# Splitting the first mixer's first weights ahead of the modulation, and putting the attention products ahead of the convolution's layer norm, in a two-block float32 kernel

## The reference

```python
mod = c_act @ w_ada[l] + b_ada[l]
sh1, sc1, ga1, sh2, sc2, ga2 = jnp.split(mod, N_MOD, axis=-1)
u = modulate(rmsnorm(h, g_norm1[l]), sh1, sc1)
...
proj = u @ w_in
p_conv, q, k, v, r, a1, gates = jnp.split(proj, offs, axis=-1)
y_conv = conv_module(p_conv, ...)      # depthwise, width 31, then layernorm, silu, @ w_pw
o = gla_chunked(q, k, v, logg)         # gated linear attention, 4 heads, value width 256
o = rmsnorm(o, g_gla_norm...)
y_gla = (o * jax.nn.silu(r)) @ w_gla_o
gt = jax.nn.sigmoid(gates)
merged = gt[:, :, 0, :] * y_conv + gt[:, :, 1, :] * y_gla
return merged @ w_out
```

## Time and profile before

| | us |
|---|---|
| median of three runs | 1522.9 |
| the three runs | 1517.42, 1522.9, 1524.58 |
| the profiled execution, its own time | 1524.56 |
| span of the profiled execution, first to last instruction | 1522.8 |
| PE, DVE, ACT busy in it | 1248.3, 676.4, 454.5 |

### The profile page before, as it was taken

How to read it: one execution, slowest core, us unless ns; L and a number is a source line. 1 busy time by engine, 2 the same in 40 slices (tenths; PEclk the granted TensorE clock), 3 DMA queues, 4 the chain that set the end, 5 groups by cost and what they waited for, 6 DMA issues and landing times.

```text
span 1522.8 us, 20505 instructions
## 1 busy us (share of the span) xinstructions
PE 1248.3 (82%) x8742; PEld 970.9 (64%) x8742; DVE 676.4 (44%) x1137; ACT 454.5 (30%) x647; POOL 1.9 (0%) x15
## 2 busy tenths in 40 slices
PE   6889988698676566566757669999999989899998
PEld 3679987587432131221212149989998879899986
DVE  2546985453300000000000055355567777667975
ACT  1533341533100000000000044343444544455453
POOL 0000000000000000000000000000000000000000
PEclk8899989899697887987778689989999989999999
DMA  9686730587999999999999947444346334445652
GB/s 356 240 281 216 220 99 1 198 279 263 391 394 398 387 398 391 395 398 388 399 389 396 396 158 229 152 139 124 126 128 191 112 111 152 136 142 174 200 206 85
DMA packets 226568, 374.51 MB, mean 246 GB/s; under 512 B 8854, under 2 KB 121896, under 8 KB 226344
## 3 DMA queue, kind: packets, MB, share of 16 engines
q1 hardware_dynamic: 226304, 369.58, 68.6%
q0 software_dynamic: 144, 3.54, 0.7%
q10 hardware_dynamic: 24, 0.03, 0.0%
HBM read 372.03 MB, written 4.62 MB: 247 GB/s over the span
## 4 chain that ended last, share of the span: by engine, by line
PE 50%; SPq 22%; DVE 13%; DMA 8%; ACT 3%; issue 3%; DVEq 0%; ACTq 0%
PE bank L554 30%; SPq L2463 22%; DVE arena L1162 5%; DMA arena<-in_w 4%; PE bank L1131 4%; DVE fine L1154 4%; DMA above<-in_w 2%; DVE arena L1154 2%; PE bank L825 2%; ACT fine L1912 2%; DMA arena<-in_w_ada 2%; PE bank L551 2%; PE bank L582 1%; ACT arena L1912 1%; PE bank L751 1%
## 5 line engine op out<-in xcount | busy, mean ns | idle before, releaser
L554 PE MATMUL bank<-fine 128*128 128x256 f32 x4656 | 587.5, 289 | 34.9 <-DVE fine L1154 24.2
L554 PEld LDWEIGHTS bank<-fine 128*128 128x128 f32 x4656 | 577.6, 197 | 44.3 <-issue 33.9
L1154 DVE TENSOR_TENSOR fine<-arena,fine 128x1024 fp32r<-128x1024 f32 (+1 forms) x257 | 299.3, 1192 | 175.3 <-ACT fine L1912 165.9
L1912 ACT ACTIVATE fine<-arena 128x1024 fp32r<-128x1024 f32 (+2 forms) x279 | 267.0, 984 | 178.7 <-PE bank L554 106.7
L1912 ACT ACTIVATE arena<-bank 128x256 f32<-128x256 f32 (+2 forms) x161 | 73.5, 482 | 606.7 <-PE bank L836 194.2
L825 PE MATMUL bank<-arena 128*32 128x512 f32 x640 | 105.7, 798 | 76.0 <-DMA arena<-in_w 76.0
L1154 DVE TENSOR_TENSOR arena<-arena,bank 128x512 f32<-128x512 f32 x8 | 5.5, 689 | 299.6 <-PE bank L825 299.6
L825 PEld LDWEIGHTS bank<-arena 128*32 128x32 f32 x640 | 20.6, 129 | 154.8 <-DMA arena<-in_w 103.1
L1912 ACT ACTIVATE arena<-arena 128x512 f32<-128x512 f32 (+6 forms) x94 | 63.3, 702 | 171.1 <-DVE arena L1154 80.4
L1162 DVE SCALAR_TENSOR_TENSOR arena<-arena 128x256 f32<-128x256 f32 (+2 forms) x265 | 108.3, 481 | 1.2 <-ACT arena L1912 0.8
L825 PE MATMUL bank<-above,arena 128*32 128x512 f32 x384 | 61.7, 778 | 39.5 <-DMA above<-in_w 39.5
(11 more groups left out here) (160 smaller groups left out, 814.0 us busy)
## 6 DMA issues: line engine op xcount, KB each, us to landing
arena<-in_w SPq DMA_DIRECT2D x240, 512.0 KB, 11.7
above<-in_w SPq DMA_DIRECT2D x144, 512.0 KB, 11.4
arena<-in_w_in SPq DMA_DIRECT2D x62, 1024.0 KB, 5.3
arena<-in_w_ada SPq DMA_DIRECT2D x24, 1024.0 KB, 7.7
arena<-in_ffn_w_up SPq DMA_DIRECT2D x22, 1024.0 KB, 5.1
arena<-in_ffn_w_down SPq DMA_DIRECT2D x11, 1024.0 KB, 4.9
arena<-in_w_ada_f SPq DMA_DIRECT2D x8, 1024.0 KB, 10.6
arena<-in_w_gla_o SPq DMA_DIRECT2D x4, 1024.0 KB, 8.5
```

Of the source, the lines that this page charges most:

```text
L554: ins = e.matmul(o, w[:, k, j * P:j * P + P], x[:, kt, :], start=start, stop=stop, skip_group_check=True)
L1154: return e.tensor_tensor(o, a, b, f)
L1912: return e.activation(o, i, f, bias=bias, scale=scale)
```

## The change

In the opening, ACT and DVE split the first weight piece (q, first 256 columns) ahead of the modulation; before, they split it after. DVE makes the low parts of u tile by tile, each right after its tile of u, instead of four tiles at a time. PE's third `ada_to_mod` comes ahead of the fourth `ada_sums`, not behind it.

At the end of the attention, PE makes the attention products first, then mu, one half of a piece, the variance, another half, the transposes, and the last half. The mean goes to bank 0 instead of the rotating banks. The scaling of the attention's output is shared: DVE scales head pair 0 of both token halves, ACT head pair 1. ACT squares the attention's output before the convolution's, after one root of a single column (eps), and ACT moves the last two pieces out later. `mod_of(1)` and `gain(1)` come later on DVE. DVE splits the first gla_o piece and makes the low parts of its activations between the four moves of the pointwise products, not after them. The first hunk only declares one more semaphore, `o_norm_a`, and is left out.

```diff
@@ -619,8 +619,8 @@
             ada_to_mod(0)
             ada_sums(2)
             ada_to_mod(1)
+            ada_to_mod(2)
             ada_sums(3)
-            ada_to_mod(2)
             ada_to_mod(3)
             advance("q", 2)
 
@@ -706,22 +706,11 @@
                                 ins = e.matmul(bank[:, j * 256:j * 256 + 256], kdT[s0:s0 + 64, tc, hh, :],
                                                v[s0:s0 + 64, tc, hh * 256:hh * 256 + 256], start=True, stop=True)
                             ins.then_inc(*states.up((c, g)))
-            bank = misc(lnorm_v, "mu")
-            e.wait_ge(*conv["taps"])
-            for m in range(4):
-                ins = e.matmul(bank[:, 0:256], ones, cacc[:, m, :], start=m == 0, stop=m == 3)
-            ins.then_inc(*ln_sum.up("mu"))
-            flush()
-            bank = take(0, lnorm_a, "rstd")
-            e.wait_ge(*lnorm_a["sq"])
-            for m in range(4):
-                ins = e.matmul(bank[:, 0:256], ones, sig[:, m, :], start=m == 0, stop=m == 3)
-            ins.then_inc(*ln_sum.up("var"))
             e.wait_ge(*masked["ps", 6, 1])
             e.wait_ge(*states_out[2, 1])
             for tc in range(2):
                 for g in range(2):
-                    bank = misc(o_norm, (tc, g))
+                    bank = misc((o_norm, o_norm_a)[g], (tc, g))
                     for j in range(2):
                         hh = 2 * g + j
                         e.matmul(bank[:, j * 256:j * 256 + 256], attn[:, tc, hh, :], v[:, tc, hh * 256:hh * 256 + 256],
@@ -732,14 +721,27 @@
                                 ins = e.matmul(bank[64 * s:64 * s + 64, j * 256:j * 256 + 256], qb[:, hh, c * 64:c * 64 + 64],
                                                St[:, c - 1, hh, :], start=False, stop=True, skip_group_check=True)
                     ins.then_inc(*o_made.up((tc, g)))
-            e.wait_ge(*o_norm[1, 1])
+            bank = take(0, lnorm_v, "mu")
+            e.wait_ge(*conv["taps"])
+            for m in range(4):
+                ins = e.matmul(bank[:, 0:256], ones, cacc[:, m, :], start=m == 0, stop=m == 3)
+            ins.then_inc(*ln_sum.up("mu"))
+            flush(2)
+            bank = take(0, lnorm_a, "rstd")
+            e.wait_ge(*lnorm_a["sq"])
+            for m in range(4):
+                ins = e.matmul(bank[:, 0:256], ones, sig[:, m, :], start=m == 0, stop=m == 3)
+            ins.then_inc(*ln_sum.up("var"))
+            flush(1)
             for tc in range(2):
                 for g in range(2):
                     bank = misc(og_out, (tc, g))
+                    e.wait_ge(*(o_norm, o_norm_a)[g][tc, g])
                     for j in range(4):
                         m = 4 * g + j
                         ins = e.transpose(bank[:, j * P:j * P + P], on[:, tc, m * P:m * P + P], ident)
                     ins.then_inc(*on_turned.up((tc, g)))
+            flush()
             e.wait_ge(*act_on["conv"])
             for m0 in range(0, 8, 2):
                 bank = misc(out_v, ("pw", m0))
@@ -1312,6 +1314,7 @@
             norm_apply(0, h)
             rows_ada(2)
             rows_ada(3)
+            advance("q", 1)
             mod_of(0, 0, 16, col("b_ada", 0, 16))
             gain(0, "g_norm1", 8)
             e.wait_ge(*mod_out["am0"])
@@ -1319,12 +1322,10 @@
                 if k % 4 == 0:
                     e.wait_ge(*normed[0, k // 4])
                 ts(u[:, k, :], sq[:, k, :], am[:, k:k + 1], ALU.mult, mod[:, k:k + 1], ALU.add).then_inc(*scaled_v.up((0, k)))
-                if k % 4 == 3:
-                    at = slice(k - 3, k + 1)
-                    e.wait_ge(*scaled_v[0, k])
-                    e.wait_ge(*x_hi_a["u1", "tile", k])
-                    tt(x_lo[0][:, at, :], u[:, at, :], x_hi[0][:, at, :].bitcast(F32), ALU.subtract).then_inc(*x_lo_v.up(("u1", k // 4)))
-            advance("q", 2)
+                e.wait_ge(*scaled_v[0, k])
+                e.wait_ge(*x_hi_a["u1", "tile", k])
+                tt(x_lo[0][:, k, :], u[:, k, :], x_hi[0][:, k, :].bitcast(F32), ALU.subtract).then_inc(*x_lo_v.up(("u1", "tile", k)))
+            advance("q", 1)
             advance("k", 1)
             e.wait_ge(*fills["a1"])
             e.wait_ge(*small_made["a1"])
@@ -1453,18 +1454,16 @@
             e.reciprocal(rs, rs).then_inc(*o_norm.up("rs"))
             e.wait_ge(*o_norm["rs"])
             for tc in range(2):
-                for g in range(2):
-                    for j in range(2):
-                        hh = 2 * g + j
-                        ins = ts(on[:, tc, hh * 256:hh * 256 + 256], bank_of(o_norm, (tc, g))[:, j * 256:j * 256 + 256],
-                                 rs[:, tc * 4 + hh:tc * 4 + hh + 1], ALU.mult)
-                    ins.then_inc(*o_norm.up((tc, g)))
-            mod_of(1, 16, 24, col("b_ada", 16, 24))
-            gain(1, "g_norm2", 32)
+                for j in range(2):
+                    ins = ts(on[:, tc, j * 256:j * 256 + 256], bank_of(o_norm, (tc, 0))[:, j * 256:j * 256 + 256],
+                             rs[:, tc * 4 + j:tc * 4 + j + 1], ALU.mult)
+                ins.then_inc(*o_norm.up((tc, 0)))
             e.wait_ge(*lnorm_a["rstd"])
             e.reciprocal(mu, mu).then_inc(*lnorm_v.up("rstd"))
             e.wait_ge(*lnorm_v["rstd"])
             tt(cacc, cacc, repeat(mu, 4), ALU.mult).then_inc(*lnorm_v.up("scaled"))
+            mod_of(1, 16, 24, col("b_ada", 16, 24))
+            gain(1, "g_norm2", 32)
             for tc in range(2):
                 for g in range(2):
                     e.wait_ge(*on_turned[tc, g])
@@ -1482,9 +1481,10 @@
                     ins = stt(gates[:, m, :], bank_of(out_v, ("pw", m0))[:, j * 256:j * 256 + 256], col("b_conv_pw", m), gates[:, m, :],
                               ALU.add, ALU.mult)
                 ins.then_inc(*out_v.up(("pw", m0)))
-            advance("gla_o", 1)
-            for g in range(2):
-                x_low("og", r, g)
+                if m0 == 0:
+                    advance("gla_o", 1)
+                elif m0 < 6:
+                    x_low("og", r, m0 // 2 - 1)
             e.wait_ge(*act_on["gates", 3])
             e.wait_ge(*out_v["pw", 6])
             advance("gla_o", 3)
@@ -2078,9 +2079,7 @@
                     for tc in range(2):
                         e.wait_ge(*kd_turned[tc])
                         act(kdT[:, tc, :, :], shaped(bank_of(kd_out, tc)[:, :], 4, P), ACT.Copy).then_inc(*kd_out.up(tc))
-            e.wait_ge(*lnorm_v["centered"])
-            act(sig, cacc, ACT.Square).then_inc(*lnorm_a.up("sq"))
-            flush()
+            act(small[:, 32:33], eps, ACT.Sqrt)
             for tc in range(2):
                 for g in range(2):
                     e.wait_ge(*o_made[tc, g])
@@ -2088,10 +2087,20 @@
                         i = tc * 4 + 2 * g + j
                         if i:
                             e.wait_ge(*o_sq.now())
-                        e.activation(junk, bank_of(o_norm, (tc, g))[:, j * 256:j * 256 + 256], ACT.Square, bias=0.0, scale=1.0,
-                                     accum_out=ss[:, i:i + 1]).then_inc(*o_sq.up(i))
+                        e.activation(junk, bank_of((o_norm, o_norm_a)[g], (tc, g))[:, j * 256:j * 256 + 256], ACT.Square, bias=0.0,
+                                     scale=1.0, accum_out=ss[:, i:i + 1]).then_inc(*o_sq.up(i))
             e.wait_ge(*o_sq[7])
             act(rs, ss, ACT.Sqrt, bias=eps, scale=1.0 / 256).then_inc(*o_sq.up("rs"))
+            e.wait_ge(*lnorm_v["centered"])
+            act(sig, cacc, ACT.Square).then_inc(*lnorm_a.up("sq"))
+            e.wait_ge(*o_norm["rs"])
+            for tc in range(2):
+                for j in range(2):
+                    hh = 2 + j
+                    ins = act(on[:, tc, hh * 256:hh * 256 + 256], bank_of(o_norm_a, (tc, 1))[:, j * 256:j * 256 + 256], ACT.Copy,
+                              scale=rs[:, tc * 4 + hh:tc * 4 + hh + 1])
+                ins.then_inc(*o_norm_a.up((tc, 1)))
+            flush(2)
             e.wait_ge(*ln_sum["var"])
             act(mu, banks[0][:, 0:256], ACT.Sqrt, bias=eps, scale=1.0 / 512).then_inc(*lnorm_a.up("rstd"))
             e.wait_ge(*lnorm_v["scaled"])
```

More of the change, by code:

```diff
@@ L452, in build @@
             "cact", "ada_rows_by_scalar", "squared_by_scalar", "rms", "scaled_by_scalar", "x_hi", "w_hi", "pieces_out_by_scalar"))
-        rep_on, softplus, decay_a, kd_out, lnorm_a, o_sq, act_on = (signal(n) for n in (
-            "bias_rows", "softplus", "decay_by_scalar", "kd_turned_out", "layer_norm_by_scalar", "o_squared", "activated"))
+        rep_on, softplus, decay_a, kd_out, lnorm_a, o_sq, o_norm_a, act_on = (signal(n) for n in (
+            "bias_rows", "softplus", "decay_by_scalar", "kd_turned_out", "layer_norm_by_scalar", "o_squared", "o_normed_by_scalar", "activated"))
         uT_out, route_a, silu_a, send_out, hidT_out, expert_a, general_a = (signal(n) for n in (
```

## The result

The changed kernel took 1497.94 us (median of 4 runs, 1496.35 to 1499.64) against 1523.67 us for the kernel before on the same occasion; the ratio is 0.984, with a 95% interval of 0.9811 to 0.9869. The forecast was 1497.0, and the time lies inside the range. The profiled execution took 1498.59 us, with a span of 1496.8: 26.0 us less than the one before.

What follows compares the result with a forecast made beforehand. PE carries half the chain; the experts' weight loading, starting at 363.84 us, shifts as a block with what precedes it. Opening 4.5 plus attention's end 21.4 gives 25.9 off 1524.56; the median, 1.7 lower, 1497.0 (own range 1491 to 1502; also 1490 to 1507).

Steps and rivals of the forecast that it cites:

- three signs: ACT's tiles at 38 or later; a wait on ACT or DVE before the pointwise products; clock 0.50 between 242 and 284.
- first two rivals: Clock drops over the transposes, 1501.1 us, chance 0.09; the opening yields nothing, 1501.5 us, chance 0.12.
- rival of no shift: Experts' stage begins by something else, or only covered work is freed: 1522.9 us, chance 0.04.
- The opening: Before 50 us: earlier q split and tile-by-tile low parts end PE's first half at 43.4; gain 4.5 us, bounds -1 to +6.5.
- rival that the opening yields nothing: DVE, stuck at q's low half, delays the modulation, or the relay gives the gain back: 1501.5 us, chance 0.12.
- The end of the attention: Loose stage, 241 to 306 us: reordered work starts the 168 products 21.4 us earlier, bounds 16 to 23.5.
- Transposes: End of the attention, after the second half: transposes taken at 3.67 us, ending at 265.3.
- Load 23: w_ada load issued at 283.0, landing 5.3 us later; PE waits 1.5 us for it before `ada_sums(11)`.
- The clock over the transposes: Rival: the clock falls during the transposes, slowing the half and pointwise bank behind; 4.1 us lost, 1501.1 us, chance 0.09.
- The layer norm as what is late next: Beside the transposes and last half: layer norm done at 266.3, 2 us to spare; rival 7 us late, 1502, chance 0.03.
- Slower, at 1.2 GHz throughout: Rival: PE stays at 1.2 GHz from 242.8 to 284, losing 34 us: 1531 us, chance 0.04.
- At nothing: Edits counted as free: early root and table load, moved `mod_of(1)` and `gain(1)`, later moves out, bank 0 for mu.

Runs made afterwards that it cites:

- f3: Changed kernel with the modulation ahead of q's second low half and one more half of gla_o's products ahead of `ada_sums(11)`: 1495.51 us, ratio 0.982.
- e1: Kernel before with the opening's edits alone: 1522.58 us against 1522.95 us, ratio 0.9993 (0.9984 to 1.0003).
- f1: Changed kernel run again without edits, on one chip with f2: 1497.58 us, ratio 0.9838 against the kernel before.
- f2: Changed kernel with the opening of before (e2 again), on one chip with f1: 1501.49 us, ratio 0.9853 against the kernel before.
- f4: Kernel before with the opening's edits alone, plus the modulation ahead of q's second low half: 1520.21 us against 1523.9 us, ratio 0.9978.
- e2: Changed kernel with the opening of before, so the end of the attention alone: 1499.83 us, ratio 0.9851 against the kernel before.
- e7: Changed kernel with each transpose of the attention's output made six times, 96 instead of 16, same result: 1514.9 us, one run.
- e8: Changed kernel with PE's layer norm sums and two halves ahead of the attention products, and ACT squaring the convolution first: 1510.46 us, one run.
- e6: Changed kernel with gla_o's low parts made after all four moves of the pointwise products, as before: 1500.17 us, one run.
- e5: Changed kernel with all four groups of the attention's output scaled on DVE, none on ACT: 1496.85 us, one run.
- e3: Changed kernel with DVE's modulation and gain ahead of q's second low half, which follows the tiles: 1494.55 us, ratio 0.9808 against before.

## Why the prediction was right

The forecast of 1497.0 missed the measured median by 0.9 us, and that closeness is luck. In the profile of after the opening left 2.0 us where 4.5 were forecast, and the end of the attention gave 23.8 where 21.4 were forecast: two errors of about 2.5 us that cancelled. The mechanism of both parts was as predicted.

Two of the three signs that the prediction named as "wrong" were in fact seen. ACT's tiles start at 38.60 ("at 38 or later"), and PE waits on ACT ahead of the pointwise products. The first goes with the 2.5 us by which the opening fell short, the second cost 0.5 us, and the range held all the same. The times of the first two rivals, 1501.1 and 1501.5, also lie inside that range, so the total alone could not have excluded them.

- **The block.** "A microsecond gained before 364 us is a microsecond off the end" held: 25.75 us between the first loads of the experts, 26.0 at the end of the span. The rival of no shift fell with it.
- **The opening**, 4.5 forecast. The order of events was as predicted, down to the modulation held behind q's low halves. A pair of tile instructions took 0.79 us (forecast 0.78), though each of the two was dearer than I took it: 0.41 and 0.43, not 0.345 and 0.38, with no gap between them. What set the first profile back is the landing of q: 34.8, not 33.1. (The columns came late too, at 35.97 instead of 34.8, but behind q's low halves that cost nothing.) Nine more profiles have q split ahead: in eight ACT starts on q between 32.98 and 33.38, in one (f3) at 35.22. So 33.1 was the usual case. With it the lead at the first 24 products is 3.2 to 4.8 us, by which profile of the old opening it is set against. The medians of the runs give less and scatter: 0.4 us in e1, 3.9 between f1 and f2 (2.6 by the means). Why is not shown. The landing of q is late in only two of ten profiles, by about 1.7 and 2.1 us, which takes some 0.4 us off a mean; and the old opening moves too, by 1.6 us between its three profiles. The rival that the opening yields nothing named the right place (DVE holding the modulation behind a transfer) and wasn't excluded by e1; f2 against f1, and f4, speak against it.
- **The end of the attention**, 21.4 forecast, 23.8 measured, twice to within 0.01 us (after and e2). The steps up to the second half held within 0.3 us: attention products 9.48 (9.5), a half 2.87 (2.92); mu and the variance took 1.92 and 1.98 (1.73 each, so 0.4 too cheap together). Three terms were too dear. *Transposes*: I took 3.67 us from the earlier trace rows, which ran at 1.2 GHz; at full clock they take 1.91, 1.8 us less. *Load 23*: I let all of `ada_sums(11)` wait for it, 1.5 us, but its first half uses load 22, and the wait was 0.4. *Hand-offs*: I charged 0.6 for eight, where PE waited once, 0.46. Against these stand mu and the variance, and the pointwise products, which took 14.05, not 13.8.
- **The clock over the transposes.** This rival came from the Trainium skill ("TensorE: Matmul & The Clock Gate", Part 4: PE-mode transpose), by which transposes don't count as busy work. Here the measurement speaks against the rival: the clock stayed at 1.00 through 10.5 us of nothing but float32 transposes (e7). Whether transposes alone would also raise a low clock, no run here shows: the sixteen of before began at 0.50 and stayed there for their 3.67 us. They were slow because the clock was already at 0.50 in the idle ahead of them, and the same sixteen took 1.91 us in after. The rival was priced with the slow row, and so, by mistake, was the forecast.
- **The layer norm as what is late next.** Right: PE's only wait in the chain there, 0.46 us, is on ACT's queue. Counted from the end of the level, PE was ready 1.6 us sooner than I took it, by the transposes above all, and the layer norm came 0.8 us later, of which mu and the variance are 0.4. That used up the 2 us of slack.
- **Slower, at 1.2 GHz throughout.** The stage has clock 1.00 from end to end. Where the clock fell in these runs' stages, PE had stood idle first: 5.05 us ahead of mu in before and e8 (then 3.75 us instead of 1.92), 2.61 us ahead of gla_o's half in e6 (then 4.60 instead of 3.13).
- **At nothing.** The shared norming really is worth 0.2 us (e5). I put the interleaved low parts at 2.6 us of wait and 1.7 of clock; without them 3.6 are lost (e6), as load 23 then hides. "Their transfers, no cost" held, but the old order shows how near they are: in e8 the weights of the pointwise products landed last, 0.3 us behind the layer norm. The earlier `o_sq[7]` of the new order keeps them off the path.

How the 23.8 us split: the order of the work 13.6 (e8), the interleaving 3.6 (e6), the sharing 0.2 (e5), each taken away alone. No run takes the other 6.4 us apart, but the profiles of before and e8, which have the same order of attention and layer norm, show where they lie. From the start of mu to the pointwise products it took 37.4 us in before (247.82 to 285.26) and 32.9 in e8 (244.11 to 276.98): 4.6 us. The pointwise products themselves took 16.04 and 14.05, as those of before began at the low clock (0.50 from 285 to 289): 2.0 us. Candidates for the 4.6, not told apart, are three. The last flush is split into single halves, one of which lies beside the layer norm. The table load of 1.28 us, in before between the last square and the root (272.57), is made early. And the scaling is shared, 1.66 us on DVE instead of 3.23.

## What to carry to other kernels

When an in-order engine idles for one late operand and then works through things that were ready all along, put the ready work first and cut the filler into pieces that fit between the dependent steps; here the order was worth more than any faster step. Take the duration of a moved step from a row at the clock that it will have in its new place. And when a split, or any filler, is put ahead of an urgent small instruction in the same queue, put only as much of it ahead as the transfer's landing leaves time for: one half instead of two ended the first products 1.4 us earlier (e3 against f1), and the runs of e3 are 3 us faster than those of f1, though on another occasion.

## What the runs showed of the hardware

At the high clock PE gets through one float32 transpose of 128 x 128 every 109 ns (10.48 us for 96 in the chain of e7), and the granted clock stays at 1.00 meanwhile. A load of 1 MB issued behind eight others of that size landed at times 1.85 us apart in two runs of the same code (ACT's start on q at 32.98 in f1, 34.83 in after), and 1.5 us of it are still there when the first mixer ends. The total times of the two profiled executions differ by 1.0 us.
